# One more group of modulation weights held ahead of each norm, and the projection stage without riders

## The chip, the cores and the metric

The kernel runs on one core of a Trainium2 chip. The metric is device time in microseconds of one execution of the whole program, as the median of several runs.

## The reference

One inference step of a two-layer backbone for two groups of tokens that share the weights: 128 context tokens and 256 latent tokens, 384 in all, width 1024. A layer is a half-step SwiGLU FFN, a parallel token mixer, and a second FFN. Each sub-layer stands between two RMS norms and is modulated by rows m[0] to m[8], which come from the conditioning vector:

```python
def modulate(x, g, shift, scale):
    return rmsnorm(x, g) * (1 + scale) + shift

def trunk_layer(x, cond, p, l, ctx, rows, cols):
    mod = jax.nn.silu(cond) @ p['ada_w'][l] + p['ada_b'][l]
    m = jnp.split(mod[:, None, :], 9, axis=-1)
    h = modulate(x, p['norm_pre'][l, 0], m[0], m[1])
    y = swiglu(h, p['ffn_gate'][l, 0], p['ffn_up'][l, 0], p['ffn_down'][l, 0])
    x = x + 0.5 * m[2] * rmsnorm(y, p['norm_post'][l, 0])
    h = modulate(x, p['norm_pre'][l, 1], m[3], m[4])
    y, new_ctx = token_mixer(h, p, l, ctx, rows, cols)
    x = x + m[5] * rmsnorm(y, p['norm_post'][l, 1])
    h = modulate(x, p['norm_pre'][l, 2], m[6], m[7])
    y = swiglu(h, p['ffn_gate'][l, 1], p['ffn_up'][l, 1], p['ffn_down'][l, 1])
    x = x + 0.5 * m[8] * rmsnorm(y, p['norm_post'][l, 2])
    return x, new_ctx
```

`ada_w` is 1024 x 9216 floats in each layer, so each of the nine rows m needs 4 MB of weights for two columns of conditioning.

## The kernel before

Activations lie transposed, features on the partitions and the 384 tokens in the free dimension: `x`, `y`, `sq`, `h_hi`, `h_lo` have eight tiles of 128 x 384 each (k = 0 to 7). Every weight is split into a high and a low part, and a product is three matmuls (high x high, high x low, low x high).

**Units.** Weights come in units of 512 KB. A unit of kind "w" is loaded by SP into one of four `raw` buffers, copied to `w_hi` by ACT (L971), subtracted to `w_lo` by POOL (L475, two instructions), and used by PE in 24 matmuls (L534). `w_hi` and `w_lo` have four slots each. A unit of kind "ada" belongs to the modulation: PE reads it straight from its buffer, in eight short matmuls (L572), and four such units make a group of 512 columns. A group is then copied to `ada_row` (ACT L1037 or DVE L1329), turned to columns by PE (`ada_turn`, L583, called by `turn_pending`), and taken to `mod` (ACT L1041 or DVE L1334). A row m is two groups, eight units.

**The order of units** is written in `PHASES`, per layer: up0 and down0 (first FFN, 44 and 24 w units), gap0, proj (12 w units), fill and merge (rest of the projections and the mixer), out (16 w units), gap1, up1, down1, and between the layers gap2. `between(units, riders, first, rest)` spreads ada units ("riders") among w units, none behind the first `first` or the last `rest`. `paired` puts the first four units (the head) in the order 0, 2, 1, 3. SP issues all loads in one order (`ALL`), in which a rider stands four w units later than in PE's order; each load waits until the one four places earlier in the ring `raw` has been used up (for w: `lo_ready`, for ada: `ada_used`).

**The gaps.** Between a sub-layer's last product and the next one's first stands a norm: PE sums squares of y (`y_sums`), ACT takes a root (`root_of_sums`, L1031), DVE inverts it (L1498) and adds the scaled y to x (`post`, L1501, L1503, L1506), ACT squares x into `sq` (L1073), PE sums those (`x_sums`, L673), ACT takes the root, DVE scales x into `y` (`times_scale`, L1440, 16 instructions), inverts the root (L1477), multiplies `y` by it into `sq` (L1480), ACT adds the shift into `h_hi` (L1080) and DVE makes `h_lo` (L1469, `low`), tile by tile. Into this time `gap` puts up to 16 ada units: 8 ahead of `x_sums`, the others behind. The first `HOLD` = 6 of them are loaded ahead into `hold`, which lies over `h_hi` and `h_lo` and is free once the stage that reads h is over; where in SP's order stands in `BEHIND` (L370 to L375), and what each waits for in `READER`. The rest go through the ring. Four gaps have 16 units; the second gap of layer 1 has 8.

**The head.** After a gap `by_tiles` runs the four head units, the first two k by k as `h_lo` becomes ready (L534 in `product`), then the third, then the fourth. Then `stream` calls `turn_pending`, which turns the gap's last group; DVE takes it in `last_group`, ahead of its first work of the next stage. In proj that work is `layer_factors` (L1750 to L1752) and `proj_out`, which evicts X0 and X1 to `proj` (L1539).

Of the kernel before, what the change touches and what calls it, by code (L numbers as in the profile page):

```python
# [10 lines left out]
T = SEQ + LAT  # L11
NB = T // 128
KT = D // 128
# [6 lines left out]
MODS = 9  # L20
MOD_TILES = MODS * KT
LAM_INIT = [0.8 - 0.6 * math.exp(-0.3 * l) for l in range(DEPTH)]
RAW, SPLIT, HOLD = 4, 4, 6

AQ, AK, AV, BQ, BI, BFF, BFB, BG, CQ, CK, CV = 0, 4, 8, 12, 16, 20, 24, 28, 32, 36, 37
P_TILES = 38
# [30 lines left out]
def build(nc, io, out):  # L57
    f32, f32r, u8 = mybir.dt.float32, mybir.dt.float32r, mybir.dt.uint8
    ALU, ACT, AX = mybir.AluOpType, mybir.ActivationFunctionType, mybir.AxisListType
    MUL, ADD, SUB = ALU.mult, ALU.add, ALU.subtract  # L60
# [5 lines left out]
    def at(name, shape, dt, offset):  # L66
        size = (int(np.prod(shape[1:])) * (1 if dt == u8 else 4) + 31) // 32 * 32
        return nc.alloc_sbuf_tensor_at(name, shape, dt, offset=offset), offset + size

    x, o = at("x", [128, KT, T], f32, base)  # L70

    hold, _ = at("hold", [128, HOLD, 1024], f32, o)
    h_hi, o = at("h_hi", [128, KT, T], f32r, o)
    h_lo, o = at("h_lo", [128, KT, T], f32r, o)
    raw, o = at("raw", [128, RAW, 1024], f32, o)
    w_hi, o = at("w_hi", [128, SPLIT, 1024], f32r, o)
    w_lo, o = at("w_lo", [128, SPLIT, 1024], f32r, o)
    R = o
    act_hi, o = at("act_hi", [128, FT, T], f32r, R)
    act_lo, R_END = at("act_lo", [128, FT, T], f32r, o)  # L80
    x_out, _ = at("x_out", [128, NB, D], f32, R)
    proj, r = at("proj", [128, P_TILES, T], f32, R)
# [23 lines left out]
    Y = R_END  # L106
    y, o = at("y", [128, KT, T], f32, Y)
    sq, o = at("sq", [128, KT, T], f32, o)
    silu, o = at("silu", [128, 2, T], f32, o)
    prod, o = at("prod", [128, 2, T], f32, o)  # L110
    Y_END = Y + 36864
    assert o <= Y_END
    y_sum, o = at("y_sum", [128, T], f32, o)
    root, o = at("root", [128, T], f32, o)
    ada_row, o = at("ada_row", [128, 512], f32, o)
    assert o <= Y_END
    rows, o = at("rows", [128, 3, 128], f32, Y)
    x_rows, o = at("x_rows", [128, NB, D], f32, o)

    first_w, o = at("first_w", [128, 16, 1024], f32, R)  # L120
    lam_in, o = at("lam_in", [128, DEPTH, 4, 64], f32, o)
    lam_p, o = at("lam_p", [128, DEPTH * 2, 64], f32, o)
    mask_f, o = at("mask_f", [128, 2, len(LEVELS), 128], f32, o)
    assert o <= R_END

    ctx_k, o = at("ctx_k", [128, 512], f32, Y)
    ctx_v, o = at("ctx_v", [128, 512], f32, o)
    ctx_kT, o = at("ctx_kT", [128, HA, 128], f32, o)
    v_nat, o = at("v_nat", [128, NB, 512], f32, o)
    k_nat, o = at("k_nat", [128, 512], f32, o)  # L130
    p = []
    for b in range(2):
        t_, o = at(f"p{b}", [128, 2, T], f32, o)
        p.append(t_)
    pT, o = at("pT", [128, 2, T], f32, o)
# [45 lines left out]
    o = Y_END  # L181
# [33 lines left out]
    with ExitStack() as ctx:  # L215
# [52 lines left out]
        def ada(L, m0, m1):  # L268

            return [Unit("ada", 4, 256, weight(io["ada_w"], L, k0 * 128, 4, g * 512 + j * 256, 256), j, k0, j + k0 == 0,  # L270
                         j == 1 and k0 == 4, "c", g, 0, 0, 0, 0, 0)
                    for g in range(2 * m0, 2 * m1) for j in range(2) for k0 in (0, 4)]
# [10 lines left out]
        def between(units, riders, first=0, rest=0):  # L283

            out_, n, r = units[:first], len(units) - first - rest, len(riders)
            for j, u in enumerate(units[first:]):
                out_.append(u)
                out_ += riders[j * r // n:(j + 1) * r // n]
            return out_

        def paired(units):

            return [units[0], units[2], units[1], units[3], *units[4:]]

        def up_units(L, f):
            u = []
            for i in range(11):
                u += halves(L, "ffn_gate", i * 256, 0, "h", ("gate", i), f=f) + halves(L, "ffn_up", i * 256, 1, "h", ("up", i), f=f)
            return u

        def down_units(L, f):
            u = []
            for j in range(4):
                u += halves(L, "ffn_down", j * 256, j % 2, "act", ("y", j), FT, f)
            return u

        def proj_units(L):
            u = []
            for j in range(6):
                u += halves(L, "w_in", j * 256, j % 2, "h", ("proj", j))  # L310
            return u
# [19 lines left out]

        PHASES, W = {"first": ada(0, 1, 2) + ada(0, 0, 1)}, []
        for L in range(DEPTH):
            riders = ada(L, 2, 5) if L == 0 else ada(L, 2, 5)[16:]
            PHASES[L, "up0"] = between(paired(up_units(L, 0)), riders[:16], SPLIT)
            PHASES[L, "down0"] = between(down_units(L, 0), riders[16:], 0, 6)
            PHASES[L, "gap0"] = ada(L, 5, 8)[:16]
            PHASES[L, "proj"] = between(paired(proj_units(L)), ada(L, 5, 8)[16:], SPLIT, 2)
            PHASES[L, "fill"] = fill_units(L)
            PHASES[L, "merge"] = merge_units(L)  # L340
            PHASES[L, "out"] = out_units(L)
            riders = ada(L, 8, 9) + (ada(L + 1, 0, 2) if L + 1 < DEPTH else [])
            PHASES[L, "gap1"] = riders[:16]
            PHASES[L, "up1"] = between(paired(up_units(L, 1)), riders[16:], SPLIT)
            PHASES[L, "down1"] = down_units(L, 1)
            if L + 1 < DEPTH:
                PHASES[L, "gap2"] = ada(L + 1, 2, 5)[:16]
# [22 lines left out]
        for name, units in PHASES.items():  # L370
            if name[1][:3] == "gap":
                last = [u for u in PHASES[name[0], {"gap0": "up0", "gap1": "fill", "gap2": "up1"}[name[1]]] if u.kind == "w"][-1]
                for j in range(HOLD):
                    BEHIND[last.n + (6 if name[1] == "gap1" else 8) + j] = (name, j)
                READER[name] = last  # L375

        order, late = [], []
# [36 lines left out]
        def raw_of(u):  # L414
            if u.raw < 0:
                return first_w[:, u.n, :]
            return hold[:, u.raw - RAW, :] if u.raw >= RAW else raw[:, u.raw, 0:u.nk * u.width]

        def slot(t, u):
            return t[:, u.split, 0:u.nk * u.width]  # L420
# [97 lines left out]
        def _(pe):  # L518
# [107 lines left out]
            def by_tiles(head):  # L626

                def part(u, k):
                    if k % 4 == 0:
                        pe.wait_ge(lo_ready[u.split], u.split_turn + 1)  # L630
                        if u.first:
                            pe.wait_ge(x_free[u.dest], seen.next(("xf", u.dest)))
                    for m in range(2):
                        mm = product(X[u.dest][:, m, 0:T], u, m, u.k0, k == 0, k == KT - 1, (k % 4,))
                    if k % 4 == 3:
                        mm.then_inc(unit_done[u.split], 1)

                for k in range(4):
                    pe.wait_ge(S["h_ready"], seen.next("h_ready"))
                    part(head[0], k)  # L640
                    part(head[1], k)
                for k in range(4, KT):
                    pe.wait_ge(S["h_ready"], seen.next("h_ready"))
                    part(head[2], k)
                for k in range(4, KT):
                    part(head[3], k)

# [661 lines left out]
        def _(dve):  # L1309
# [119 lines left out]
            def marked(ins):  # L1429

                ins.then_inc(S["dve_step"], 1)
                return seen.next("dve_step")

            GROUPS = list(enumerate(((0, SEQ), (SEQ, T))))

            def times_scale():

                for k in range(KT):
                    for g, (t0, t1) in GROUPS:
                        ins = V.tensor_scalar(y[:, k, t0:t1], x[:, k, t0:t1], mA[:, k, g:g + 1], None, MUL)  # L1440
                return marked(ins)

            def first_pre():

                dve.wait_ge(S["root_ready"], seen.next("root_ready"))
# [20 lines left out]
            def low(k):  # L1466
                dve.wait_ge(S["hh_ready"], seen.next("hh_ready"))
                for g, (t0, t1) in GROUPS:
                    ins = V.scalar_tensor_tensor(h_lo[:, k, t0:t1], sq[:, k, t0:t1], mB[:, k, g:g + 1],  # L1469
                                                 h_hi[:, k, t0:t1], ADD, SUB)  # L1470
                ins.then_inc(S["h_ready"], 1)

            def pre():
                made = times_scale()
                dve.wait_ge(S["root_ready"], seen.next("root_ready"))
                dve.wait_ge(S["dve_step"], made)
                step(V.reciprocal(root[:, :], root[:, :]))  # L1477

                for k in range(KT):
                    V.tensor_tensor(sq[:, k, :], y[:, k, :], root[:, :], MUL).then_inc(S["norm_ready"], 1)  # L1480
                    if k:
                        dve.wait_ge(S["norm_ready"], seen.next("my_norm"))
                        low(k - 1)
                dve.wait_ge(S["norm_ready"], seen.next("my_norm"))
                low(KT - 1)

# [469 lines left out]
```

## Time and profile before

| | us |
|---|---|
| median of 3 runs | 2445.39 (2443.46 to 2450.45) |
| profiled execution | 2440.73 |
| its span in the profile | 2438.9 |
| mean granted clock of TensorE, share of full | 0.969 |
| PE busy | 2271.4 (93%) |
| DVE, ACT, POOL busy | 968.0, 902.8, 1268.9 |
| loads of ada_w: ring / held / at the start | 98 / 30 / 16, of 512 KB |

Times below are microseconds from the start of the span. PE's matmul records overlap their neighbours, so the time of a stretch of products is read from the chain, not by adding means. X, S and Ab are PSUM tiles; a name like `S L572` is the line and what it writes.

### The profile page before, as it was taken

The numbers are of one execution on the slowest core, as the hardware profiler recorded it, in microseconds if no ns is written. First come the engines' busy times: TensorE is split into PE (matmuls) and PEld (weight loads), VectorE is DVE, ScalarE is ACT, GpSimd is POOL, SyncE is SP. The second block draws the span as 40 slices with busy tenths as digits, with TensorE's granted clock in tenths as the row PEclk, the third lists the DMA queues.
The fourth block names the chain that finished last, engine by engine and source line by source line (L and its number), as shares of the span: only waits on it lengthen the run. The fifth ranks groups of instructions, "written<-read, shape, count | busy, mean of one in ns | idle before, by whom it ended". The sixth has DMA issues, their size and how long they took to land.

```text
span 2438.9 us, 33514 instructions
## 1 busy us (share of the span) xinstructions
PE 2271.4 (93%) x13833; PEld 2124.3 (87%) x13833; DVE 968.0 (40%) x1586; ACT 902.8 (37%) x1219; POOL 1268.9 (52%) x988
## 2 busy tenths in 40 slices
PE   7999998998988898999999999889898988989998
PEld 5999977896888897999979999789787988889997
DVE  4211233435677546122152121515366763632212
ACT  3222332244744354222242232313556535433231
POOL 2666543343477453666636666344335863546663
PEclk8999998998999999999999999999999999999998
DMA  8555645432222345445454445553222223534431
GB/s 265 164 156 161 210 155 173 130 87 65 72 67 61 95 148 156 138 147 160 156 154 144 147 134 190 169 157 95 72 77 64 78 70 93 175 87 130 121 123 67
DMA packets 362223, 311.93 MB, mean 128 GB/s; under 512 B 9923, under 2 KB 359383, under 8 KB 362071
## 3 DMA queue, kind: packets, MB, share of 16 engines
q1 hardware_dynamic: 354967, 304.01, 40.9%
q10 hardware_dynamic: 7104, 5.77, 0.7%
q8 instruction: 110, 1.80, 0.3%
q14 instruction: 42, 0.34, 0.0%
HBM read 305.81 MB, written 3.93 MB: 127 GB/s over the span
## 4 chain that ended last, share of the span: by engine, by line
PE 77%; DVE 10%; ACT 6%; DMA 2%; issue 2%; POOL 1%; SPq 1%; ACTq 0%; DVEq 0%
PE X L534 52%; PE S L534 8%; PE Ab L534 7%; DMA raw<-in_ada_w 2%; PE X L791 2%; PE S L572 1%; PE Ab L572 1%; PE S L583 1%; ACT w_hi L971 1%; PE X L716 1%; POOL w_lo L475 1%; DVE y L1501 1%; PE S L745 1%; DVE x L1503 1%; ACT p L1127 1%
## 5 line engine op out<-in xcount | busy, mean ns | idle before, releaser
L475 POOL TENSOR_TENSOR w_lo<-raw,w_hi 128x512 fp32r<-128x512 f32 (+1 forms) x872 | 1167.9, 1360 | 1098.4 <-ACT w_hi L971 1093.2
L971 ACT ACTIVATE w_hi<-raw 128x1024 fp32r<-128x1024 f32 (+1 forms) x436 | 453.3, 1041 | 825.9 <-PE X L534 759.9
L534 PE MATMUL X<-h_hi,w_hi 128*128 128x384 f32 x1600 | 548.2, 343 | 15.6 <-DVE h_lo L1469 9.7
L534 PE MATMUL X<-h_lo,w_hi 128*128 128x384 f32 x1600 | 541.6, 338 | 0.0
L534 PE MATMUL X<-h_hi,w_lo 128*128 128x384 f32 x1600 | 540.8, 338 | 0.0
L534 PEld LDWEIGHTS X<-h_hi,w_hi 128*128 128x128 f32 x1600 | 305.4, 191 | 36.4 <-issue 25.7
L534 PEld LDWEIGHTS X<-h_lo,w_hi 128*128 128x128 f32 x1600 | 305.8, 191 | 0.0
L534 PEld LDWEIGHTS X<-h_hi,w_lo 128*128 128x128 f32 x1600 | 305.5, 191 | 0.0
L1512 DVE TENSOR_TENSOR prod<-X,silu 128x768 f32<-128x768 f32 x44 | 42.1, 958 | 539.7 <-PE X L534 539.6
L534 PE MATMUL X<-act_hi,w_hi 128*128 128x384 f32 x704 | 236.8, 336 | 0.0
L534 PE MATMUL X<-act_hi,w_lo 128*128 128x384 f32 x704 | 235.3, 334 | 0.0
L534 PE MATMUL X<-act_lo,w_hi 128*128 128x384 f32 x704 | 235.3, 334 | 0.0
L1523 DVE TENSOR_SCALAR y<-X,mG 128x128 f32<-128x128 f32 x96 | 33.4, 410 | 319.4 <-ACT prod L1095 319.4
L534 PE MATMUL Ab<-h_hi,w_hi 128*128 128x384 f32 x400 | 141.9, 355 | 13.0 <-DVE gates L1384 6.8
L534 PE MATMUL S<-h_hi,w_hi 128*128 128x384 f32 x400 | 140.0, 350 | 0.0
L534 PE MATMUL Ab<-h_lo,w_hi 128*128 128x384 f32 x400 | 136.3, 341 | 0.0
L534 PEld LDWEIGHTS X<-act_hi,w_hi 128*128 128x128 f32 x704 | 132.2, 188 | 4.5 <-issue 4.5
L534 PE MATMUL Ab<-h_hi,w_lo 128*128 128x384 f32 x400 | 136.1, 340 | 0.0
L534 PE MATMUL S<-h_lo,w_hi 128*128 128x384 f32 x400 | 135.2, 338 | 0.0
L534 PE MATMUL S<-h_hi,w_lo 128*128 128x384 f32 x400 | 135.1, 338 | 0.0
L534 PEld LDWEIGHTS X<-act_lo,w_hi 128*128 128x128 f32 x704 | 132.2, 188 | 0.0
L534 PEld LDWEIGHTS X<-act_hi,w_lo 128*128 128x128 f32 x704 | 132.2, 188 | 0.0
(336 smaller groups left out, 3336.7 us busy)
## 6 DMA issues: line engine op xcount, KB each, us to landing
raw<-in_w_in SPq DMA_DIRECT2D x124, 512.0 KB, 3.8
raw<-in_ada_w SPq DMA_DIRECT2D x98, 512.0 KB, 3.6
raw<-in_ffn_gate SPq DMA_DIRECT2D x88, 512.0 KB, 3.8
raw<-in_ffn_up SPq DMA_DIRECT2D x88, 512.0 KB, 3.8
raw<-in_ffn_down SPq DMA_DIRECT2D x80, 512.0 KB, 3.4
hold<-in_ada_w SPq DMA_DIRECT2D x30, 512.0 KB, 4.6
first_w<-in_ada_w SPq DMA_DIRECT2D x16, 512.0 KB, 8.9
raw<-in_w_out SPq DMA_DIRECT2D x16, 512.0 KB, 3.5
```

Of the source, the lines that this page charges most:

```text
L475: ins = nc.gpsimd.tensor_tensor(slot(w_lo, u)[:, part], raw_of(u)[:, part], slot(w_hi, u)[:, part], SUB)
L534: mm = nc.tensor.matmul(dst, w[:, k, m * 128:m * 128 + 128], r_, start=start and k + j == 0, stop=stop and k == u.nk - 1 and j == 2)
L572: mm = nc.tensor.matmul(G[g % 2][32 * k:32 * k + 32, u.dest * 256:u.dest * 256 + 256], c_col[:, u.k0 + k, :], w[:, k, :], start=u.k0 == 0, ...
L583: mm = nc.tensor.matmul(S6[:, 2 * m:2 * m + 2], ada_row[:, m * 128:m * 128 + 128], con[:, C_SEL:C_SEL + 2], start=True, stop=True)
L716: mm = nc.tensor.matmul(X[n % 2][:, c, at_:at_ + k.shape[-1]], proj[64 * c:64 * c + 64, (AQ if kind == "a" else CQ) + h, b * 128:b * 128 + ...
L745: mm = nc.tensor.matmul((S5, S6)[c][:, 0:128], v, pT[:, c, j * 128:j * 128 + 128], start=j == 0, stop=j == len(kbs) - 1)
L791: mm = nc.tensor.matmul(X[n % 2][:, j // 4, j % 4 * 128:j % 4 * 128 + 128], g, g, start=True, stop=True)
L971: A(slot(w_hi, u), raw_of(u), ACT.Copy).then_inc(hi_ready[u.split], 1)
L1127: e = A(p[n % 2][:, c, 0:w], X[n % 2][:, c, 0:w], ACT.Exp, bias=nmax[:, n % 2, c:c + 1], accum_out=esum[:, n % 2, c:c + 1])
L1501: step(V.tensor_tensor(y[:, t, :], y[:, t, :], wide(root[:, :], 2), MUL))
L1512: V.tensor_tensor(prod[:, :, :], X[1][:, :, 0:T], silu[:, :, :], MUL).then_inc(x_free[1], 1)
L1523: ins = V.tensor_scalar(y[:, 2 * i + m, t0:t1], X[u.dest][:, m, t0:t1], mG[:, 2 * i + m, g:g + 1], None, MUL)
```

## The change

- `HOLD` is 9. Three more buffers, `hold_sq`, lie over `sq`; held units 0 to 2 go there, 3 to 8 to the six of `hold`. In the second gap of layer 1, which has 8 units, all 8 are held.
- In the gap behind the mixer the held loads begin 4 instead of 6 w units behind the last unit of fill, in SP's order.
- The row m[5], 8 ada units, is computed with the riders of the first FFN: up0 has 24 riders in layer 0 (16 before) and 16 in layer 1 (8 before); down0 has 8 in layer 0 and none in layer 1, as before. gap0 has the 16 units of m[6] and m[7] (before m[5] and m[6]), and proj has none (before the 8 of m[7]).
- `by_tiles` calls `turn_pending` between the third and the fourth head unit.
- `pre` scales four tiles of x ahead of the wait for the root, and one of the others after each of the multiplications 1 to 4 by the root.

```diff
-RAW, SPLIT, HOLD = 4, 4, 6
+RAW, SPLIT, HOLD = 4, 4, 9
...
-    hold, _ = at("hold", [128, HOLD, 1024], f32, o)
+    hold, _ = at("hold", [128, 6, 1024], f32, o)
...
+    hold_sq, _ = at("hold_sq", [128, 3, 1024], f32, o - KT * T * 4)
...
-            riders = ada(L, 2, 5) if L == 0 else ada(L, 2, 5)[16:]
-            PHASES[L, "up0"] = between(paired(up_units(L, 0)), riders[:16], SPLIT)
-            PHASES[L, "down0"] = between(down_units(L, 0), riders[16:], 0, 6)
-            PHASES[L, "gap0"] = ada(L, 5, 8)[:16]
-            PHASES[L, "proj"] = between(paired(proj_units(L)), ada(L, 5, 8)[16:], SPLIT, 2)
+            riders = ada(L, 2, 6) if L == 0 else ada(L, 2, 6)[16:]
+            PHASES[L, "up0"] = between(paired(up_units(L, 0)), riders[:24], SPLIT)
+            PHASES[L, "down0"] = between(down_units(L, 0), riders[24:], 0, 6)
+            PHASES[L, "gap0"] = ada(L, 6, 8)
+            PHASES[L, "proj"] = paired(proj_units(L))
...
-                for j in range(HOLD):
-                    BEHIND[last.n + (6 if name[1] == "gap1" else 8) + j] = (name, j)
+                for j in range(min(HOLD, len(units))):
+                    BEHIND[last.n + (4 if name[1] == "gap1" else 8) + j] = (name, j)
...
-            return hold[:, u.raw - RAW, :] if u.raw >= RAW else raw[:, u.raw, 0:u.nk * u.width]
+            if u.raw >= RAW:
+
+                return hold_sq[:, u.raw - RAW, :] if u.raw < RAW + 3 else hold[:, u.raw - RAW - 3, :]
+            return raw[:, u.raw, 0:u.nk * u.width]
...
                     part(head[2], k)
+                turn_pending()
                 for k in range(4, KT):
                     part(head[3], k)
...
             def pre():
-                made = times_scale()
+                made = {}
+
+                def times_scale(k):
+                    for g, (t0, t1) in GROUPS:
+                        ins = V.tensor_scalar(y[:, k, t0:t1], x[:, k, t0:t1], mA[:, k, g:g + 1], None, MUL)
+                    made[k] = marked(ins)
+
+                def times_root(k):
+                    dve.wait_ge(S["dve_step"], made[k])
+                    V.tensor_tensor(sq[:, k, :], y[:, k, :], root[:, :], MUL).then_inc(S["norm_ready"], 1)
+
+
+                for k in range(4):
+                    times_scale(k)
                 dve.wait_ge(S["root_ready"], seen.next("root_ready"))
-                dve.wait_ge(S["dve_step"], made)
                 step(V.reciprocal(root[:, :], root[:, :]))
-
-                for k in range(KT):
-                    V.tensor_tensor(sq[:, k, :], y[:, k, :], root[:, :], MUL).then_inc(S["norm_ready"], 1)
-                    if k:
-                        dve.wait_ge(S["norm_ready"], seen.next("my_norm"))
-                        low(k - 1)
+                times_root(0)
+                for k in range(1, KT):
+                    times_root(k)
+                    if k + 3 < KT:
+                        times_scale(k + 3)
+                    dve.wait_ge(S["norm_ready"], seen.next("my_norm"))
+                    low(k - 1)
                 dve.wait_ge(S["norm_ready"], seen.next("my_norm"))
                 low(KT - 1)
```

## Rows read from the trace of the kernel before

**Rows 1.** Busy time of each engine, the page's part 1.
```profile
PE 2271.4 (93%) x13833; PEld 2124.3 (87%) x13833; DVE 968.0 (40%) x1586; ACT 902.8 (37%) x1219; POOL 1268.9 (52%) x988
```
**Rows 2.** Waits of PE, whole span: total us, times, longest.
```profile
PE S L572 <- DMA raw<-in_ada_w: 21.8, 15, 2.5
...
PE X L534 <- DVE h_lo L1469: 9.7, 2, 6.3
```
**Rows 3.** Chain of waits in layer 0's proj: start, us, what.
```profile
375.79 18.17 PE X L534 x96
393.95 0.80 PE S L583 x8
...
396.60 0.97 DVE proj L1539
...
397.70 6.00 PE X L534 x24
...
409.89 2.54 POOL w_lo L475 x2
...
412.45 3.54 DMA raw<-in_ada_w
...
448.69 1.11 PE X L689 x8
```
**Rows 4.** Chain in layer 1's proj, its first and last step.
```profile
1577.64 18.00 PE X L534 x96
...
1647.08 1.11 PE X L689 x8
```
**Rows 5.** Chain in the second FFN of layer 0, then of layer 1.
```profile
953.26 17.90 PE X L534 x96
...
1150.69 87.48 PE X L534 x504
...
1238.17 0.02 issue
...
2143.13 276.49 PE X L534 x1584
```
**Rows 6.** Chain: first products of layer 0's first FFN, and its end.
```profile
45.42 31.92 PE X L534 x168
...
348.92 0.02 issue
```
**Rows 7.** Waits of PE from 40 to 330 us, those for riders.
```profile
PE S L572 <- DMA raw<-in_ada_w: 0.4, 1, 0.4
PE Ab L572 <- DMA raw<-in_ada_w: 0.3, 1, 0.3
```
**Rows 8.** Timeline of layer 0's second gap, PE's late units, SP's loads.
```profile
941.76 1.93 PE L572 MATMUL Ab<-raw,c_col 128*32 128x256 f32 x32
...
942.46 2.02 SPq L438 DMA_DIRECT2D raw<-in_ada_w  x4
...
950.75 1.08 PE L572 MATMUL S<-raw,c_col 128*32 128x256 f32 x8 [2.27 <-DMA raw<-in_ada_w]
...
952.17 1.08 PE L572 MATMUL S<-raw,c_col 128*32 128x256 f32 x8 [0.34 <-DMA raw<-in_ada_w]
```
**Rows 9.** Timeline of layer 1's second gap, DVE, ACT and PE behind the x sums.
```profile
2134.39 3.76 DVE L1440 TENSOR_SCALAR y<-x,mA 128x128 f32<-128x128 f32 x16
...
2136.09 0.58 ACT L1031 ACTIVATE root<-S,eps 128x384 f32<-128x384 f32 x1 [1.18 <-PE S L673]
...
2138.25 2.55 DVE L1477 RECIPROCAL root<-root 128x384 f32<-128x384 f32 x1
...
2142.99 0.55 DVE L1480 TENSOR_TENSOR sq<-y,root 128x384 f32<-128x384 f32 x1
2143.13 0.69 PE L534 MATMUL X<-h_hi,w_hi 128*128 128x384 f32 x1 [6.29 <-DVE h_lo L1469]
2143.46 0.74 DVE L1469 SCALAR_TENSOR_TENSOR h_lo<-sq,mB,h_hi 128x128 fp32r<-128x128 f32 x2
```

More of the change, by code:

```diff
@@ L1434, in _ @@
             GROUPS = list(enumerate(((0, SEQ), (SEQ, T))))
-            def times_scale():
-                for k in range(KT):
-                    for g, (t0, t1) in GROUPS:
-                        ins = V.tensor_scalar(y[:, k, t0:t1], x[:, k, t0:t1], mA[:, k, g:g + 1], None, MUL)
-                return marked(ins)
             def first_pre():
@@ L1473, in pre @@
             def pre():
-                made = times_scale()
+                made = {}
[8 more added lines that the diff above has]
+                    times_scale(k)
                 dve.wait_ge(S["root_ready"], seen.next("root_ready"))
-                dve.wait_ge(S["dve_step"], made)
                 step(V.reciprocal(root[:, :], root[:, :]))
-                for k in range(KT):
-                    V.tensor_tensor(sq[:, k, :], y[:, k, :], root[:, :], MUL).then_inc(S["norm_ready"], 1)
-                    if k:
-                        dve.wait_ge(S["norm_ready"], seen.next("my_norm"))
-                        low(k - 1)
+                times_root(0)
[5 more added lines that the diff above has]
+                    low(k - 1)
                 dve.wait_ge(S["norm_ready"], seen.next("my_norm"))
```

## The prediction, made before the changed kernel was run

> **What bounds the kernel now.** I read the page first, then the waits of PE, then the chain of waits stage by stage. PE is busy for 93% of the span [rows 1]. So this kernel gains where PE stands idle or runs at the lower clock behind an idle stretch, and loses by what is added to PE's queue. The waits of PE that this change can reach are: loads of modulation weights (21.8 us on the one PSUM bank) and the first rows of h (9.7 us) [rows 2]. Nearly all of this sits in the five norms between sub-layers and in the two projection stages.
>
> The stage "proj" of layer 0 runs from the first product to the first transpose of the mixer: 448.69 − 375.79 = 72.90 us [rows 3]. It holds 12 weight units of 24 products. PE at full clock needs 87.48 / 504 × 24 = 4.17 us for one [rows 5], so 50 us are products and 23 us are something else. The chain names it: a turn of the last modulation group behind the fourth unit, DVE's take, its layer factors and only then the first eviction, all before the fifth unit starts at 397.70; that unit takes 6.00 us instead of 4.17, a lower clock. Then w_lo on POOL, behind it the load of a rider (3.54 us), and PE waiting for it; this pattern is there a second time 20 us later. Layer 1 has the same stage with 1647.08 − 1577.64 = 69.44 us [rows 4].
>
> **Projections without riders.** What stays: the four head units (18.17 us, low clock at their start included), the turn (0.80 us), eight units at 4.17 (33.3 us) and some 1.2 us of last eviction before the mixer (the eviction takes 0.97 us, issue around it): 53.5 us in layer 0. Layer 1: 18.00 + 0.80 + 33.3 + 1.2 = 53.3 us. Removed: 72.9 − 53.5 = 19.4 and 69.4 − 53.3 = 16.1, together **35.5 us** [rows 3, 4].
>
> This counts the DVE stall as gone, which is the work of the earlier turn. The turn now stands in PE's queue ahead of the fourth head unit (4.17 us of products), so it ends near 390.6 instead of 394.75; DVE's take and factors last from 394.75 to 396.60, 1.8 us [rows 3], and end near 392.4; the eviction of X0 ends near 393.5, before the fourth unit does. The turn itself waits for ACT's copy of ada_row. ACT comes to that right behind the last h_hi, while PE still has four k of the third unit to do, so I cost the wait at nothing; were the cover gone, it would cost the copy and the take, under 1 us each. If the edit bought nothing, the DVE stall (397.70 − 394.75 = 3 us, and 1.8 us for the slow unit behind it) would stay in both layers: 9.6 us less gain.
>
> **Eight riders more in each up0.** They don't vanish, they move. Layer 0's second FFN, with 8 riders and their two turns, runs from 953.26 to 1238.17 = 284.91 us; layer 1's, with none, takes 276.49 us [rows 5]. The difference of 8.4 less the head's turn (0.8) is 7.6 us per eight. Layer 0's first FFN, with 24 riders, took 348.92 − 45.42 = 303.5 [rows 6], so 27.0 us over the same 276.5, 9.0 per eight with everything that happens at the kernel's start. I take 8.0 per eight: **16.0 us** added, bounds 15.2 and 18.0.
>
> That holds only if the riders find their weights landed. The rider behind unit j is loaded behind unit j + 4, in a ring of four. With at most one rider in the two places ahead of it, its buffer is the one that unit j + 2 leaves, whose w_lo is done about 3.8 us after PE ends unit j − 2 and whose successor has landed 3.6 us later: 7.4 us. (In the chain: w_lo starts at 409.89, 1.2 us behind the products, the DMA starts at 412.45 and takes 3.54.) PE needs the rider after two units and a rider, 2 × 4.17 + 0.8 = 9.1 us: 1.7 us to spare. Two riders behind one unit, as proj had, take away that margin, and there PE waited. Layer 0's up0 now has 24 riders on 40 units, in the order 0, 1, 0, 1, 1; layer 1's has 16 on 40, which is what layer 0's had before. In both, a rider has at most one in the two places ahead, so the margin is that of before, where all of layer 0's up0 and down0 showed 0.7 us of waiting for such loads [rows 7].
>
> **Nine held units instead of six.** In a gap with 16 units, 9 to 12 now land in the ring early, and only 13, 14 and 15 are loaded behind the x sums, instead of 12 to 15. Take layer 0's second gap. Before: PE starts unit 8 at 941.76, SP issues the four loads over 2 us from 942.46, PE starts the third of them at 950.75, the fourth at 952.17, each right at its landing, and the head units at 953.26 [rows 5, 8]. After: unit 8 is a held one, so the first of the late loads is issued one unit (1.93 / 4 = 0.48 us) later, and the last one to land is the third. So the last unit starts 1.4 us earlier less 0.48, about 1.0 us. Four gaps have this form: **4.0 us**. Bounds: nothing, if another load shares the engines in the same time, and 2.4 us each (9.6) if landings follow at 1.5 us from a first load of 3.6 us. I take the low value, since it is the measured spacing of the same transfers.
>
> The Trainium skill, "DMA: Bandwidth & Descriptors", Specifications and Anatomy of one DMA, gives some 2 us fixed and about 358 GB/s from memory to one core, by which the third of three loads of 512 KB would land 6.4 us after the first issue. The row shows 8.3 us for the third of four [rows 8]. By the page each gap would give 2.8 us, the sum would be 7 us better; the row decides.
>
> The three further held loads ride in stretches where loads already come in pairs with down0's riders: I take 0.5 us against, bounds 0 and 3. Behind the mixer the first held load is two units sooner in SP's queue, and it waits for the last fill unit. All later loads, those of w_out, queue behind it. They are needed only after four merge units of 4 us each, which cover a 3.6 us load, ACT and POOL; cost nothing.
>
> **The scaling around the root.** In the four full gaps PE waits for loads longer than for h, so DVE's new order is free: h comes every 1.7 us for k of 1 to 4 (0.55 for root, 0.74 for h_lo, 0.47 for two scalings) instead of 1.1 [rows 9], and PE needs 12 products, 2.1 us, per k there. In layer 1's second gap, with 8 units, PE waited 6.29 us for the first h_lo [rows 9]. There DVE's 16 scalings run for 3.76 us from 2134.39, while ACT's root is ready at 2136.67. With 8 of them first, DVE is free at 2136.27 and the reciprocal starts at 2136.75 instead of 2138.25 [rows 9]; the fifth scaling fits in the 0.47 us in which DVE waits for ACT's first h_hi. **1.5 us**, once; bounds 0.5 and 1.5.
>
> **Sum.** 35.5 − 16.0 + 4.0 + 1.5 − 0.5 = 24.5 us off. The profiled execution took 2440.73 us (span 2438.9, under 2 us around it), so 2416.2 by its own time. The median of the runs is 2445.39, 4.7 us over it; I predict for the median, 2445.4 − 24.5 = **2421 us**, −1.0%.
>
> The Trainium skill, "TensorE: Matmul & The Clock Gate", Part 1, says that an idle stretch throws the array back to half clock until it was busy again. The rows agree (6.00 us for a unit of 4.17, 18.17 for a head of 16.7). If the shorter wait in a gap kept the clock, each head would give 1.5 us more; loads still stop PE between the last units, so I don't count it.
>
> **The rivals.**
> - A, forecast, −24.5 us, 2421, own range 2411 to 2431, chance 0.73.
> - B, the loads come later than reckoned where riders stand behind neighbouring units. Up0 of layer 0 has eight such pairs. At the price of a stop in proj (1.9 us idle and 1.3 us of lower clock) they cost 8 × 3.2 = 26 us: 2447, no change. For it: proj's stops, and held loads that already stretch the landing. Against: the 1.7 us to spare. 0.07.
> - C, slower: in the same stage both riders of each group 1, 1 stop PE, and POOL's w_lo falls behind because its raw buffers are released late: 16 × 3.2 = 51 us, against a gain of 24.5: 2472. It decides from 1.5 us lost per rider. For that the loads would have to take more than 5.4 us instead of 3.5 [rows 3]. Four loads at once took as long (third load of [rows 8]); in up0 one or two are under way. 0.03.
> - D, the gaps give most of what they can: 9.6 instead of 4.0, and cheaper riders (15.2): 2414, inside the range. 0.09.
> - E, the DVE stall stays: the turn waits, or DVE is still late for X0. 9.6 us less, with gaps at nothing 13.6: 2431 to 2435. 0.08.
>
> **How the numbers follow.** Range: 2411 (D with 3 us of spread between runs) to 2435 (E); it leaves out B, C and some of A's edge. Within 0.3% (7.3 us, about what a measurement of this kernel can tell from no change): B and the upper end of E, 0.08. Slower: C and part of B, 0.05. Faster: 0.87.
>
> **What would show it.** Both proj stages at 53 to 54 us with no wait for in_ada_w; the chain passing from the fourth head unit straight to the fifth; up0 of layer 0 and 1 longer by 8 us each, waits there below 2 us; the head units of the four full gaps 1 us sooner after the x sums; the reciprocal of the last gap 1.5 us sooner. Waits for loads in up0 above 5 us, or a fifth unit that still starts behind DVE, would make the prediction wrong.

## The result, and the profile after

The changed kernel takes 2419.95 us (median of 4 runs, 2415.86 to 2422.49) against 2447.92 us of the kernel before beside it: ratio 0.9886, 95% interval 0.9863 to 0.9909. Run again on another occasion (below) it took 2421.45 us, ratio 0.9915 (0.989 to 0.9939). So the change takes 21 to 28 us off; 24.5 was forecast, and 2421 us as the time. That the median lies 1 us from it is in part luck: the forecast was reckoned from 2445.39 us, and the kernel before took 2447.92 beside the changed one.

The page after, part 1, beside [rows 1]:

```profile
PE 2267.5 (94%) x13833; PEld 2121.7 (88%) x13833; DVE 967.9 (40%) x1586; ACT 902.8 (37%) x1219; POOL 1270.3 (52%) x988
```

The same number of instructions, nearly the same busy time; what is shorter is the span. The waits of PE over the whole span, beside [rows 2]:

```profile
PE S L576 <- DMA raw<-in_ada_w: 14.7, 15, 1.9
...
PE X L538 <- DVE h_lo L1467: 8.2, 2, 4.7
...
PE Ab L576 <- DMA raw<-in_ada_w: 0.5, 1, 0.5
```

The eviction to `proj`, on which PE had stood in both layers, is no longer in the list. In the kernel before it was there with two waits:

```profile
PE X L534 <- DVE proj L1539: 5.9, 2, 3.0
```

The chain of waits in layer 0's proj, whole, beside [rows 3] (start, us, what):

```profile
383.40 13.63 PE X L538 x72
397.03 0.79 PE S L587 x8
397.82 37.57 PE X L538 x216
435.38 0.02 issue
435.41 0.97 DVE proj L1550
...
436.48 0.55 PE X L694 x3
```

Where 55 steps with ACT, POOL, DVE and the DMA engines among them had stood, there are three head units, the turn, and nine units in one piece: 216 products in 37.57 us, 4.17 us a unit. The stage takes 436.48 − 383.40 = 53.08 us. Layer 1, beside [rows 4]:

```profile
1572.26 14.73 PE X L538 x72
1586.98 0.79 PE S L587 x8
1587.77 37.56 PE X L538 x216
...
1626.43 1.11 PE X L694 x8
```

54.17 us. The timeline shows the cover that the sooner turn was to give DVE, here in layer 0:

```profile
396.87 0.95 PE L587 MATMUL S<-con,ada_row 128*128 128x2 f32 x8
...
397.86 0.17 DVE L1339 COPY mod<-S 128x8 f32<-128x8 f32 x1 [10.16 <-PE S L587]
...
399.52 0.16 DVE L1763 TENSOR_SCALAR lbl<-omlb 128x8 f32<-128x8 f32 x1
399.71 0.96 DVE L1550 TENSOR_SCALAR proj<-X 128x768 f32<-128x768 f32 x1
```

PE doesn't wait ahead of the turn, DVE takes the group and is through with the factors in 1.85 us, and X0 is evicted at 400.67, ahead of the end of the fourth unit (397.82 + 4.17 = 401.99).

The stages as the chain gives them, in us. A stage runs from its first product to the end of its last, a gap from there to the next stage's first product; "mixers" end where the last long run of products in out starts, and that run, 29.4 us before and after, is left out:

| stage | before | after | difference | forecast |
|---|---|---|---|---|
| first FFN, layer 0 | 303.52 | 312.40 | +8.9 | +8.5 |
| first FFN, layer 1 | 286.02 | 293.00 | +7.0 | +8.0 |
| proj, layer 0 | 72.90 | 53.08 | −19.8 | −19.4 |
| proj, layer 1 | 69.44 | 54.17 | −15.3 | −16.1 |
| four full gaps | 26.85, 27.80, 26.72, 26.71 | 25.60, 26.20, 26.74, 25.37 | −4.2 | −4.0 |
| last gap | 22.32 | 20.77 | −1.6 | −1.5 |
| second FFNs | 284.93, 276.51 | 285.59, 277.50 | +1.6 | 0 |
| mixers | 447.33, 444.28 | 449.43, 447.24 | +5.1 | 0 |

The terms of the sum come to −25.0 us. The span fell only by 18.2, since the mixers and the second FFNs were longer in this profile. The experiments explain the second FFN of layer 1 and a part of the mixers.

### The profile page after: what moved, and what is told of

It is laid out like the page before. It is cut to its first block, busy times and chain, and to the rows that moved or that the text cites. A ratio compares the mean times of both kernels' runs of the same rounds, so it can differ in the third digit from the quotient of the medians.

```text
span 2420.7 us, 33510 instructions
## 1 busy us (share of the span) xinstructions
PE 2267.5 (94%) x13833; PEld 2121.7 (88%) x13833; DVE 967.9 (40%) x1586; ACT 902.8 (37%) x1219; POOL 1270.3 (52%) x988
## 4 chain that ended last, share of the span: by engine, by line
PE 77%; DVE 10%; ACT 6%; issue 2%; DMA 2%; SPq 1%; POOL 1%; ACTq 0%; DVEq 0%
PE X L538 52%; PE S L538 8%; PE Ab L538 7%; PE X L796 2%; DMA raw<-in_ada_w 2%; PE S L576 1%; PE Ab L576 1%; PE S L587 1%; PE X L721 1%; PE S L750 1%; DVE x L1514 1%; DVE y L1512 1%; ACT w_hi L976 1%; ACT p L1132 1%; SPq L456 1%
## 5 line engine op out<-in xcount | busy, mean ns | idle before, releaser
L538 PE MATMUL Ab<-h_hi,w_hi 128*128 128x384 f32 x400 | 142.3, 356 | 12.9 <-DVE gates L1389 6.8
```

What stands on the lines that cost most here:

```text
L538: mm = nc.tensor.matmul(dst, w[:, k, m * 128:m * 128 + 128], r_, start=start and k + j == 0, stop=stop and k == u.nk - 1 and j == 2)
```

## The experiments

**Is the sooner turn worth anything without riders in proj?**

```diff
                     part(head[2], k)
-                turn_pending()
```

> The changed kernel with one edit undone: the turn of the last modulation group stands behind the fourth head unit again. My theory (the sooner turn lets DVE take the group and compute the layer factors while PE still has a unit to do): each proj stage is longer by the DVE stall and the slow unit behind it, 3.0 + 1.6 us, so 57.7 instead of 53.1 us in layer 0 and 58 in layer 1, together 9 us; the up stages don't change. Against the changed kernel about +9 us. Rival (without riders in proj the stall would have gone anyway, the turn gives nothing): 0 us, both stages stay at 53 to 54.

Measured: 2427.96 us, ratio to before 0.9934 (0.9919 to 0.9949). The changed kernel did not run beside it; by the two ratios of that kernel, the late turn costs 5 to 12 us. The proj stages take 60.00 and 60.03 us. The chain of waits in layer 0:

```profile
402.56 0.80 PE S L587 x8
...
405.20 0.97 DVE proj L1549
406.17 0.14 issue
406.31 36.20 PE X L538 x192
```

and the windows before and behind that start (busy time of PE, PEld, DVE, ACT, POOL, granted clock, DMA share, GB/s):

```profile
402.50:406.30 3.80, 0.84 (x9) 0.78 (x8) 2.64 (x11) 1.06 (x1) 2.50 (x2) 0.86 0.48 148
406.30:410.00 3.70, 3.69 (x12) 3.70 (x13) 0.96 (x1) 0.00 (x0) 0.00 (x0) 0.50 0.48 142
```

The stall is back with the same 3 us (403.36 to 406.31), and behind it the array runs at half clock, 1.2 GHz: eight units take 36.20 us instead of 33.3. So one late turn costs 3.0 + 2.9 us here, not 3.0 + 1.6. The next run has the same late turn and the same stall of 2.9 us, but more clock in the windows behind it:

```profile
404.60:408.00 3.40, 3.39 (x12) 3.40 (x13) 0.96 (x1) 0.00 (x0) 0.00 (x0) 0.57 0.55 156
408.00:410.00 2.00, 2.00 (x12) 2.00 (x11) 0.00 (x0) 0.00 (x0) 0.00 (x0) 0.87 0.00 0
```

Its eight units take 35.1 us in both layers, 1.8 over 33.3, as the prediction had it. The slow part behind one and the same stall thus cost 1.8 us in one program and 2.9 in the other.

**What do the riders alone give?**

```diff
-            PHASES[L, "gap0"] = ada(L, 5, 8)[:16]
-            PHASES[L, "proj"] = between(paired(proj_units(L)), ada(L, 5, 8)[16:], SPLIT, 2)
+            PHASES[L, "gap0"] = ada(L, 6, 8)
+            PHASES[L, "proj"] = paired(proj_units(L))
```

with the riders of up0 and down0 as in the change, and the rest as before.

> The kernel before with the riders moved and nothing else (six held units, late turn, scaling ahead of the root). My theory: proj falls from 72.9 and 69.4 us to 57.7 and 58, since only the DVE stall stays (together -27 us), both first FFNs grow by 8 us, gaps stay: -10 to -11 us against before. Rival (moving riders only shifts the work and its waits, the gain comes from the held units and the turn): within 3 us of before.

Measured: 2430.95 us, ratio 0.9945 (0.9928 to 0.9962). Proj takes 57.39 and 58.15 us, the first FFNs 312.18 and 293.04: −26.8 and +15.7, 11 us off by the stages, as expected, and 14 by the medians (the kernel before took 2444.78 us beside it). Moving riders gives nearly half of the gain, and it needs neither held units nor the turn. Against this run the changed kernel's proj stages are another 7.0 to 8.3 us shorter together, against the run with the late turn 11.5 to 12.8: that is what the sooner turn is worth.

**What do the held units alone give?** The kernel before with `HOLD` = 9, `hold_sq` and the place 4 behind the mixer.

> The kernel before with nine held units and the earlier place of the held loads behind the mixer, and nothing else. My theory: three instead of four loads come behind the x sums, each full gap is 1.0 to 1.5 us shorter, 4 to 5 us in all; the stage in which the three more held loads arrive loses at most 1 us. Rival (the gap ends with the last landing, which only depends on when PE has used the ring): 0 us. Second rival (the earlier held load behind the mixer blocks SP and makes the mixer longer): the mixer stages grow by 2 to 3 us as in the profile of the changed kernel.

Measured: 2437.44 us (2432.79 to 2440.92) against 2444.78 us, ratio 0.997 (0.9957 to 0.9983). The four full gaps take 26.00, 26.58, 25.48 and 25.49 us, 4.5 less than before together; the first FFN of layer 0, in which more held loads arrive, 302.39 (303.52 before). The mixers take 446.99 and 444.71 us. So the loads held ahead give their 1.1 us a gap and cost nothing that the stages show (the medians differ by 7.3 us), and the sooner place in SP's queue does not lengthen the mixer.

**What does the scaling alone give?** The kernel before with the new `pre`.

> The kernel before with only the scaling of x divided around the root. My theory: the reciprocal starts 1.5 us sooner in all gaps, but only the second gap of layer 1, where PE waits for h, is shorter, by 1.5 us; the four full gaps stay within 0.3 us. Rival (the slower pace of h, 1.6 instead of 1.1 us a tile, makes PE wait in the head units): head units longer by 1 us or more each, no gain. Time against before: -1.5 us by my theory, 0 to +5 by the rival.

Measured: ratio 0.9979 (0.9961 to 0.9997), 2440.95 us (2433.13 to 2447.74); a spread of 14 us between runs says little on 1.5, the rows do. The last gap takes 20.77 us instead of 22.32, as forecast. The four full gaps take 27.75, 26.91, 26.64 and 27.17 us, 0.4 more than before together; singly they are up to 0.9 us off either way, where I had expected 0.3. And the stage behind the last gap takes 277.48 instead of 276.51. No wait stands in the head units, so the slower pace of h is not it. The granted clock is: first the changed kernel, then the kernel before, 8.1 us from the first product:

```profile
2123.90:2132.00 8.10, 8.10 (x31) 8.10 (x32) 8.08 (x24) 4.65 (x12) 0.00 (x0) 0.65 0.00 0
```

```profile
2143.10:2151.20 8.10, 8.07 (x37) 8.07 (x38) 7.48 (x20) 5.98 (x13) 0.00 (x0) 0.78 0.00 0
```

In the kernel before, products came every 0.32 us for 3.4 us and then every 0.17; in the changed kernel and in this one they did so for 5.6 us. Shorter windows show why: in both kernels the granted clock stands at 0.50 for 6.8 us, from 2139.9 to 2146.7 before and from 2122.8 to 2129.6 in the changed kernel. Before, PE was idle for 3.3 of these, ahead of the head; now for 1.1 only, and the head has the rest. So 1.0 of the 1.5 us is given back. All seven profiles with the new `pre`, those below included, show it (277.2 to 277.6 us), all three with the old one 276.51. The Trainium skill, "TensorE: Matmul & The Clock Gate", Part 1, says that the default state is throttled and that activity releases the throttle. The trace agrees in that PE stood idle before the clock fell and ran products before it rose.

**Does the ring's margin hold the forecast for up0?** The changed kernel with the 24 riders of layer 0 on 18 units instead of 40, as dense as proj had them.

```diff
-            PHASES[L, "up0"] = between(paired(up_units(L, 0)), riders[:24], SPLIT)
+            PHASES[L, "up0"] = between(paired(up_units(L, 0)), riders[:24], SPLIT, 22 if L == 0 else 0)
```

> The changed kernel with layer 0's 24 riders of up0 on 18 units, as dense as proj had them (1, 1, 2 behind successive units), instead of on 40. Same work. My theory (a second rider behind one unit is loaded too late for the ring of four): six places with two riders, each with a stop of 1.9 us and 1.3 us of lower clock: layer 0's first FFN longer by 15 to 20 us. Rival (riders were costly in proj for another reason, the evictions there): 0 to 3 us longer.

Measured: 2438.11 us (2433.79 to 2443.35), 17 us slower than the changed kernel beside it. Layer 0's first FFN takes 335.05 us instead of 312.40, 22.6 more, where 15 to 20 was expected; the profile is that of the slowest of its ten runs. One period of its chain:

```profile
90.02 4.40 PE X L538 x24
...
94.50 1.07 ACT w_hi L976
...
95.63 2.54 POOL w_lo L479 x2
...
98.19 3.53 DMA raw<-in_ada_w
...
101.76 0.64 PE S L576 x8
102.40 5.95 PE X L538 x24
```

This is the pattern of [rows 3], with nearly the same durations: unit, w_hi, w_lo, load, 7.3 us in all, while PE has one unit and two riders to do. It comes at each of the six double places, with 5.4 to 6.0 us for the unit behind. 22.6 / 6 = 3.8 us a place; I had reckoned 3.2. With the same 24 riders and no two behind one unit, PE waits 1.5 us in all for riders (in the changed kernel, 45 to 365 us; 1.8 in its second profile):

```profile
PE S L576 <- DMA raw<-in_ada_w: 1.0, 3, 0.4
...
PE Ab L576 <- DMA raw<-in_ada_w: 0.5, 1, 0.5
```

So rivals B and C are answered by the mechanism: what stops PE is two riders behind one unit, not a rider behind each of two neighbours.

**Is the longer mixer part of the change?** Two runs: the changed kernel with the held loads behind the mixer begun 6 units late again, and the changed kernel once more.

```diff
-                    BEHIND[last.n + (4 if name[1] == "gap1" else 8) + j] = (name, j)
+                    BEHIND[last.n + (6 if name[1] == "gap1" else 8) + j] = (name, j)
```

> The changed kernel with the held loads behind the mixer begun six units behind the last fill unit, as before, instead of four. My theory: no difference; mixer stages between 444 and 449 us as in all profiles so far, gap behind it 26 us. Rival (the mixer was 2 to 3 us longer in the profile of the changed kernel because SP stands at the first held load sooner): mixer stages 2 to 3 us shorter in both layers.

> The changed kernel once more, beside the others, to see how much one profile differs from the next. My theory: gaps, FFNs and proj stages within 1 us of the first profile, mixer stages anywhere from 444 to 449 us. Rival (the longer mixer belongs to the change): mixer stages again at 447 and 449 us.

Measured: 2420.51 us, ratio 0.9907 (0.9882 to 0.9933), and 2421.45 us, ratio 0.9915 (0.989 to 0.9939). Mixers 447.07 and 447.37 us with the late place, 447.09 and 447.58 with the changed kernel again. So the place in SP's queue is not it. In layer 0 the mixer took 445.6 to 449.4 us over ten profiles, and 449.4 and 447.1 in two of the same program: scatter. Where I followed it, between the first profiles of before and after, most of it is in the recurrence: three runs of 12, 12 and 24 products take 2.93, 3.08 and 5.97 us instead of 2.32, 2.08 and 4.43, with no longer wait ahead of them. The granted clock was 1.00 in all three before and 0.76, 0.68 and 0.71 after. In layer 1 my expectation missed: four profiles with all edits, or all but the place, lie at 447.2 to 447.6 us, the others at 444.3 to 446.9. The last experiment, with all edits and shorter gaps, has 443.1 there, so the edits don't make it longer in every case; why these four are longer stays open. In this second profile of the changed kernel the full gaps take 25.81, 26.23, 25.30 and 25.40 us: the third, which hadn't moved in the first profile, is 1.4 us shorter too, more than the 1 us that I had allowed. Its third load landed 7.1 us after SP's first issue here, 8.6 in the first profile.

**What bounds the gap now?** A full gap still ended on loads. The changed kernel, gap of layer 0 behind the mixer, beside [rows 8]:

```profile
931.31 0.64 PE L576 MATMUL Ab<-hold,c_col 128*32 128x256 f32 x8
...
932.45 2.39 SPq L442 DMA_DIRECT2D raw<-in_ada_w  x3
...
938.29 1.06 PE L576 MATMUL S<-raw,c_col 128*32 128x256 f32 x8 [0.77 <-DMA raw<-in_ada_w]
...
940.48 1.08 PE L576 MATMUL S<-raw,c_col 128*32 128x256 f32 x8 [1.12 <-DMA raw<-in_ada_w]
```

Three loads instead of four, the last landed 8.0 us after the first issue (8.3 for the third of four before), at 9.2 us behind the start of unit 8 instead of 10.4. The Trainium skill, "DMA: Bandwidth & Descriptors", has about 358 GB/s from memory to one core (Specifications) and some 2 us fixed, fitted for DMAs that GpSimd issues (Anatomy of one DMA), while SP issues these. An estimate from its figures is 6.4 us; in the eight full gaps of the changed kernel's two profiles it was 7.1 to 8.6 us, so the trace is above it. h is ready well before that: in layer 0's first gap the first h_lo is there at 378.5, and the head starts at 383.4. So the last three units got buffers of their own over the activations' region, free from the last unit of the stage ahead of the gap:

```diff
+    hold_r, _ = at("hold_r", [128, LAST, 1024], f32, R)
...
+            elif name in OVER and j >= 16 - LAST:
+                ALL[g] = PHASES[name][j] = PHASES[name][j]._replace(raw=RAW + HOLD + j - 16 + LAST,
+                                                                   raw_turn=list(OVER).index(name))
...
-                        reader = READER[u.raw_turn]
+                        reader = (READER if u.raw < RAW + HOLD else OVER)[u.raw_turn]
```

> The changed kernel, with the last three ada units of each full gap (13 to 15) loaded into buffers of their own over the activations' region, which is free from the last unit of the stage ahead of the gap on; nothing waits for the ring behind the x sums. My theory (in a full gap the last landing is what holds the head units, h is ready earlier): PE reaches the head at the first h_lo, which in the changed kernel stood at 378.5 in the first gap, against the head's start at 383.4; each full gap falls from about 26 to about 21.5 us, 4 x 4.5 = 18 us against the changed kernel, some of it given back where the clock rises no sooner, so -14 to -18 us, near 2403. Rival (the norm's own chain or PE's ada units end as late as the loads do): gaps stay above 25 us, less than 4 us.

Measured: 2394.48 us (2391.64 to 2395.47), ratio to before 0.9804 (0.978 to 0.9828), 27 us faster than the changed kernel beside it, and the fastest version of this study. Each full gap takes 21.1 us. Its chain in layer 0, from the x sums on:

```profile
370.24 3.02 PE S L690 x8
373.26 0.79 PE S L599 x8
374.05 1.91 PE Ab L588 x32
...
375.98 0.60 ACT ada_row L1054
...
376.63 1.05 PE S L599 x8
377.68 1.43 PE S L588 x24
379.12 5.92 PE X L550 x33
```

No DMA in it: PE's own short matmuls and one copy by ACT are the bound now. The gaps give 19.5 us against the first profile of the changed kernel and 18.4 against the second, as expected. The time missed my range all the same: 27 us, where I had said 14 to 18, with some loss at the clock. Against the second profile, whose span is 29.3 us longer, the stages behind the full gaps give 6.8 us, 1.1 to 2.4 each, and the mixers 4.1. For the stages the windows show the cause. First the last part of layer 0's first gap and the head behind it in the changed kernel:

```profile
375.80:383.40 7.60, 4.62 (x41) 1.65 (x33) 7.55 (x23) 4.45 (x11) 0.00 (x0) 0.68 0.99 321
383.40:391.40 8.00, 8.00 (x42) 8.00 (x42) 4.01 (x11) 2.95 (x8) 0.00 (x0) 0.87 0.65 219
```

then the whole gap and the head here:

```profile
358.00:379.10 21.10, 18.66 (x175) 10.19 (x174) 18.48 (x30) 10.13 (x21) 4.16 (x4) 1.00 0.55 175
379.10:387.10 8.00, 8.00 (x49) 8.00 (x47) 7.79 (x24) 4.85 (x14) 0.00 (x0) 1.00 0.48 156
```

In the changed kernel the clock falls to half in every full gap, while PE waits for the late loads. Here PE has no such wait, and the clock stays at 1.00 through all four and the heads behind them; the prediction had put that at 1.5 us a head, and not counted it. In the last gap, where PE still waits for h, it falls as before. The mean over the span was 0.976 to 0.981 in the five runs of this kernel, 0.969 to 0.975 in the eight of the changed one. What made the mixers shorter wasn't followed.

## Why the prediction was right

- **Projections without riders, −35.5.** Right: −35.1 in the first pair of profiles. Scatter stands beside it: the stage of the kernel before took between 69.3 and 72.9 us over three kernels that share it, the new one between 53.1 and 54.6 (52.1 and 52.9 in the last experiment). Both stages together took 140.5 to 142.3 us before and 107.3 to 108.6 after, so pairs of profiles give 32 to 35 us, and 35.1 is the upper end.
- **The turn covers DVE.** Right, by the two runs with the late turn. I said 9.6 us for both layers, with 1.8 us of slow unit each; the stages say 11.5 to 12.8 with all other edits, where the slow clock cost 2.9 us a stall, and 7.0 to 8.3 by the run with riders alone, where it cost 1.8. The sum took the stage as a whole and does not depend on it.
- **Riders in up0, +16.0, and 0.5 for held loads.** Right: +8.9 and +7.0, 15.9 against 16.5. The argument for the ring's margin, which put rivals B and C at a tenth together, was tested by bunching, and holds: a rider behind each of two neighbours does not stop PE, a second rider behind one unit does.
- **Gaps, −4.0.** Right in mechanism and size: −4.2 and −5.3 in two profiles, −4.5 for the held units alone. Rival D asked for landings 1.5 us apart from 3.6 us on, so the third at 6.6; it came at 7.1 to 8.6. (Its working gives 2.6 us a gap, 10.5 in all, not 2.4 and 9.6.)
- **The root, −1.5.** The gap gives it (2118.40 for ACT's root, DVE at 2119.01 instead of 1.5 us later), and 1.0 of it is lost in the head behind. The prediction took the whole 1.5 us as gain. I had not looked at what the clock does with a head that starts sooner; the miss is too small for the sum to show it.

The rows of the last gap after, beside [rows 9]:

```profile
2116.70 1.92 DVE L1476 TENSOR_SCALAR y<-x,mA 128x128 f32<-128x128 f32 x8
...
2118.40 0.58 ACT L1036 ACTIVATE root<-S,eps 128x384 f32<-128x384 f32 x1 [1.18 <-PE S L678]
2119.01 2.55 DVE L1487 RECIPROCAL root<-root 128x384 f32<-128x384 f32 x1 [0.39 <-ACT root L1036]
...
2123.89 0.69 PE L538 MATMUL X<-h_hi,w_hi 128*128 128x384 f32 x1 [4.75 <-DVE h_lo L1467]
```

DVE now waits 0.39 us for the root, so ACT's root is the bound of this step and no more scaling need be moved.

## What to carry to other kernels

Find the place where side work goes in twice behind one unit of the main work: in a ring as deep as the look-ahead, the second load of a pair arrives too late, and the same work spread one by one is nearly free of waits (1.5 us for 24 riders). Price a stall of PE with the products behind it, here 3 us of waiting and 1.8 to 2.9 us of slower clock. And where a wait for loads ends a stage, look for memory that is dead just then: three buffers over it gave as much again as the whole change.

## What the runs showed of the hardware

- Starting the array 1.5 us sooner after an idle stretch gave only 0.5 us: the clock stood at half for 6.8 us either way, and products stayed at 0.32 us for 5.6 instead of 3.4 us.
- With no wait for loads behind the x sums the granted clock stayed at 1.00 through four gaps of 21.1 us and the heads behind them; with such waits, in gaps of 25 to 28 us, it fell to half in each.
- The same stall of 3 us ahead of the fifth unit cost 1.8 us of slower clock in one program and 2.9 in another.
- Two executions of the same program had 449.4 and 447.1 us for the same mixer. Between two different programs, most of such a difference lay in products at the lower clock (0.68 to 0.76 instead of 1.00), not in a wait.
